# Modulation weights of a two-layer stack: the conditioning product moved from GpSimd and TensorE to VectorE

## The reference

```python
def modulate(h, shift, scale):
    return h * (1.0 + scale) + shift
...
    c_act = jax.nn.silu(c)
    cc_act = jax.nn.silu(c_ctx)
...
        mod = (c_act @ ada_w[l] + ada_b[l])[:, None, :]
        sh1, sc1, g1, sh2, sc2, g2 = jnp.split(mod, N_MOD, axis=-1)
        h = modulate(x, sh1, sc1)
        if need_ctx:
            mod_c = cc_act @ ada_w[l] + ada_b[l]
...
        x = layer_norm(DEEPNORM_ALPHA * x + g1 * y, ln_g[l, 0], ln_b[l, 0])
        h = modulate(x, sh2, sc2)
        x = layer_norm(DEEPNORM_ALPHA * x + g2 * sq_relu_mlp(h, mlp_w1[l], mlp_w2[l]), ln_g[l, 1], ln_b[l, 1])
```

## Time and profile before

| | |
|---|---|
| median of 3 runs | 2835.18 us (2833.04 to 2839.2) |
| profiled execution | 2831.1 us |
| its span | 2829.0 us |
| granted TensorE clock, mean | 0.975 |
| TensorE busy | 2687.7 us, 95% |
| VectorE busy | 1546.7 us, 55% |
| ScalarE busy | 1037.2 us, 37% |
| GpSimd busy | 875.1 us, 31% |

### The profile page before, as it was taken

How to read it: one execution, slowest core, us unless ns; L and a number is a source line. 1 busy time by engine, 2 the same in 40 slices (tenths; PEclk the granted TensorE clock), 3 DMA queues, 4 the chain that set the end, 5 groups by cost and what they waited for, 6 DMA issues and landing times.

```text
span 2829.0 us, 39455 instructions
## 1 busy us (share of the span) xinstructions
PE 2687.7 (95%) x13346; PEld 2210.4 (78%) x13346; DVE 1546.7 (55%) x2275; ACT 1037.2 (37%) x1648; POOL 875.1 (31%) x648
## 2 busy tenths in 40 slices
PE   7999999999999999999989798889999899899997
PEld 6886788887889988888768476678877777788886
DVE  7754554546567755454552774464455655644445
ACT  5234322223347732222331365452233422433323
POOL 2320554543331155445220200144543442300002
PEclk9999999999999999999989899999999999899998
DMA  4121344443300034443412000124444133122222
GB/s 140 67 82 45 127 137 146 140 140 134 133 31 2 2 129 138 141 148 134 142 60 89 8 1 1 52 82 141 135 140 132 69 133 119 62 102 97 97 95 77
DMA packets 77272, 272.27 MB, mean 96 GB/s; under 512 B 8304, under 2 KB 11632, under 8 KB 76784
## 3 DMA queue, kind: packets, MB, share of 16 engines
q1 hardware_dynamic: 58560, 205.55, 21.4%
q10 hardware_dynamic: 18608, 65.34, 6.8%
HBM read 268.75 MB, written 2.10 MB: 96 GB/s over the span
## 4 chain that ended last, share of the span: by engine, by line
PE 80%; DVE 10%; ACT 5%; issue 3%; DMA 1%; POOL 0%; DVEq 0%; ACTq 0%; SPq 0%
PE banks L2175 58%; PE banks L2330 5%; DVE w_lo L1301 3%; PE banks L2627 2%; PE banks L2734 2%; PE banks L2235 2%; PE banks L2719 2%; PE banks L2595 1%; PE banks L2610 1%; ACT w_hi L704 1%; PE banks L2364 1%; PE banks L2699 1%; DVE ffn_hid L2099 1%; DVE attn_nm L1922 1%; PE banks L2624 0%
## 5 line engine op out<-in xcount | busy, mean ns | idle before, releaser
L2175 PE MATMUL banks<-h_hi,w_hi 128*128 128x512 f32 x1616 | 644.9, 399 | 26.8 <-DVE w_lo L1301 21.3
L2175 PE MATMUL banks<-h_lo,w_hi 128*128 128x512 f32 x1616 | 633.2, 392 | 0.0
L2175 PE MATMUL banks<-h_hi,w_lo 128*128 128x512 f32 x1616 | 631.8, 391 | 0.0
L704 ACT ACTIVATE w_hi<-w_raw 128x1024 fp32r<-128x1024 f32 x371 | 389.8, 1051 | 573.6 <-PE banks L2175 452.9
L1301 DVE TENSOR_TENSOR w_lo<-w_raw,w_hi 128x1024 fp32r<-128x1024 f32 x371 | 522.3, 1408 | 140.6 <-ACT w_hi L704 127.7
L2175 PE MATMUL banks<-g_hi,w_hi 128*128 128x512 f32 (+1 forms) x1120 | 437.7, 391 | 13.4 <-DVE w_lo L1301 8.7
L2175 PE MATMUL banks<-g_lo,w_hi 128*128 128x512 f32 (+1 forms) x1120 | 429.2, 383 | 0.0
L2175 PE MATMUL banks<-g_hi,w_lo 128*128 128x512 f32 (+1 forms) x1120 | 428.5, 383 | 0.0
L520 POOL TENSOR_TENSOR ada_raw<-ada_raw,c_act 128x1024 f32<-128x1024 f32 x112 | 220.9, 1972 | 646.3 <-DMA ada_raw<-ada 646.0
L2175 PEld LDWEIGHTS banks<-h_hi,w_hi 128*128 128x128 f32 x1616 | 305.3, 189 | 103.3 <-DVE w_lo L1301 31.9
L2175 PEld LDWEIGHTS banks<-h_hi,w_lo 128*128 128x128 f32 x1616 | 305.2, 189 | 65.0
(11 more groups left out here) (398 smaller groups left out, 3704.8 us busy)
## 6 DMA issues: line engine op xcount, KB each, us to landing
w_raw<-weights SPq DMA_DIRECT2D x384, 512.0 KB, 3.2
ada_raw<-ada ACTq DMA_DIRECT2D x112, 512.0 KB, 3.4
x<-x SPq DMA_DIRECT2D x4, 512.0 KB, 6.8
out<-x SPq DMA_DIRECT2D x8, 256.0 KB, 2.2
mix_cum<-ret_tab ACTq DMA_DIRECT2D x1, 1024.0 KB, 4.9
nsa_w<-cmp_w ACTq DMA_DIRECT2D x1, 1024.0 KB, 7.2
nsa_cbias<-nsa_cbias ACTq DMA_DIRECT2D x1, 1024.0 KB, 9.6
attn_ctx<-ctx ACTq DMA_DIRECT2D x1, 1024.0 KB, 6.8
```

What stands on the lines that cost most here:

```text
L704: act.activation(w_hi[s][:], w_raw[s][:], ACT.Copy).then_inc(w_hi_done, 1)
L2175: mm = pe.matmul(bank, w[s][:, k, :], m[:, k, :], start=(n == 0 and a == 0), stop=(n == kts - 1 and a == 2))
```

## The change

A job's weights are laid out the other way round: the 128 outputs lie on the partitions and the 1024 inputs along the row. The SiLU of `c` and `c_ctx` is then wanted as a row that is the same on all partitions: `c_row` (128 x 2 x 1024), loaded already repeated, with the SiLU on ScalarE (`silu_of_rows`). It lies in memory that other stages overwrite, so it is loaded again, `c` alone, before out1 and before out2. A job becomes one instruction of VectorE, `tensor_tensor_reduce` with product and sum into `ada_col` (128x1), and the addition of the bias from there. GpSimd's and TensorE's parts are taken out.

Places move too: nsa_in and attn_in carry no jobs any more, nor do the first pair of out1 and the second pair of mlp0_up0; in their stead all 4 pairs of ffn0_down2, 2 of ffn1_down2 and 2 of mlp0_down3 carry one. In a pair the load is issued behind ScalarE's first split, and VectorE's part comes between the second split and the second body, in front of which it waits for the load. In out0, out1 and mlp0_up0 ScalarE runs the SiLU before the second body of a pair, in out0 and out1 with the table of the square root loaded again behind it. The core of the diff:

```diff
-ADA_STAGES = ["out0", "nsa_in", "out1", "attn_in", "conv_in"]
-ADA_STAGES += [n for n, _ in PLAN if (n[:3] == "ffn" and n[4:] != "_down2") or (n[:4] == "mlp0" and n[4:] != "_down3")]
-ADA_FIRST = {"attn_in": 6, "mlp0_up0": 1, "conv_in": 1}
+ADA_STAGES = ["out0", "out1", "conv_in"] + [n for n, _ in PLAN if n[:3] == "ffn" or n[:4] == "mlp0"]
+ADA_FIRST = {"out1": 1, "mlp0_up0": 2, "conv_in": 1}
+ADA_PAIRS = {n: {"ffn1_down2": 2, "mlp0_down3": 2}.get(n, PAIRS[n] - ADA_FIRST.get(n, 0)) for n, _ in PLAN
+             if n in ADA_STAGES}
...
-            def condition(a, who):
-
-                pool.wait_ge(ada_loaded, 16 * a + 16)
-                vector = c_act[:, :, who:who + 1].broadcast_to([P, KT, P])
-                pool.tensor_tensor(ada_raw[:], ada_raw[:], vector, ALU.mult).then_inc(ada_step, 1)
...
             def load_ada(...):
-                    act.wait_ge(ada_added, a + 1)
+                    if not isinstance(a, int) or a > 0:
+                        act.wait_ge(ada_done, a)
...
+            def silu_of_rows(rows, n):
+
+                act.wait_ge(row_in, 16 * n)
+                act.activation(rows, rows, ACT.Silu).then_inc(c_silu, 1)
...
                 with act.Fori(p0, p1 - tail) as i:
                     for s in range(2):
                         split_next(i, s)
-                        if s:
+                        if s == 0:
                             load_ada(name, i, first)
...
             first_residual = scaled_squares(1, "ffn0")
-            table_of_sqrt()
             p0 = PAIR0["out0"]
+            load_ada("out0", p0, 0)
             first_residual(p0, 0, 0)
             split_next(p0, 1)
-            load_ada("out0", p0, 0)
+            silu_of_rows(c_row[:], 1)
+            table_of_sqrt()
             first_residual(p0, 1, 1)
...
+                    if not isinstance(a, int) or a > 0:
+                        dve.wait_ge(ada_taken, a)
+                    dve.wait_ge(ada_loaded, 16 * a + 16)
+                    dve.tensor_tensor_reduce(ada_raw[:], ada_raw[:], c_row[:, who, :], 1.0, 0.0, ALU.mult, ALU.add,
+                                             ada_col[:]).then_inc(ada_done, 1)
                     dve.wait_ge(ada_done, a + 1)
-                    dve.tensor_scalar(mod[:, bass.ds(a - skipped, 1), who], psum[5][:, 0:1],
+                    dve.tensor_scalar(mod[:, bass.ds(a - skipped, 1), who], ada_col[:],
...
                 with dve.Fori(p0, p1 - tail) as i:
                     for s in range(2):
                         split_next(i, s)
+                        if s:
+                            take_ada(name, i, first)
                         body(i, s, 2 * (i - PAIR0[name]) + s)
-                    take_ada(name, i, first)
...
-            def ada_unit(name, i, first):
-
-                if with_ada(name, first):
-                    a = i - ada_skipped(name)
-                    pe.wait_ge(ada_added, a + 1)
-                    if not isinstance(a, int) or a > 0:
-                        pe.wait_ge(ada_taken, a)
-                    pe.matmul(psum[5][:, 0:1], ada_sum[:, 0, :], ones[:, 0:1], start=True, stop=True)\
-                        .then_inc(ada_done, 1)
```

More of the change, by code:

```diff
@@ L75 @@
 assert _c == ADA_JOBS and ADA_JOB0["ffn0_up1"] == ADA_CTX
-ADA_BEFORE_NSA = ADA_JOB0["nsa_in"] + 4
-ADA_BEFORE_ATT = ADA_JOB0["attn_in"]
+ADA_BEFORE_ATT = ADA_JOB0["mlp0_up0"]
 def with_ada(name, first=0):
-    if name not in ADA_JOB0 or name == "nsa_in" and first > 3:
+    if name not in ADA_JOB0:
         return False
-    return first == 6 if name == "attn_in" else first >= ADA_FIRST.get(name, 0)
+    return 0 <= first - ADA_FIRST.get(name, 0) < ADA_PAIRS[name]
 def ada_skipped(name):
```

159 lines of the change are left out of this document (70 added, 89 removed).

## The result

| | before | after |
|---|---|---|
| median of the runs | 2834.15 us (2833.04 to 2839.2) | 2795.11 us (2790.92 to 2801.81) |
| ratio, 95% interval | | 0.9861 (0.9842 to 0.988) |
| profiled execution, its span | 2831.1, 2829.0 | 2797.2, 2795.4 |
| TensorE busy | 2687.7 | 2660.7 |
| VectorE busy | 1546.7 | 1595.2 |

The account below looks back on a forecast made before the run. TensorE's matmuls, and its waits for the low halves of weights made by VectorE, were taken as the bound. 26.2 + 17.8 - 11.4 = 32.6 us off 2831.1 gave 2798.5 profiled, a median of 2802.6, range 2791 to 2825.

Parts of the forecast that it names:

- TensorE's matmul, 26.2 us: On TensorE in all pairs with jobs: removing 112 jobs at 0.234 us each saves 26.2 us.
- GpSimd beside VectorE, 17.8 us: First MLP, conv_in and elsewhere: VectorE no longer slowed by GpSimd, saving 8.0, 6.8 and 3.0 us, 17.8 in all.
- elsewhere: Openings of nsa_in, attn_in and the ffn stages: 3.0 us saved, an estimate bounded by 0 and 6.
- The length of the product-and-sum, 1.24 us: On VectorE, each job: the new instruction over 128x1024 takes 1.24 us, in a block of 1.55 us.
- the case of the half rate: Rival, VectorE: product-and-sum some 2.3 us, blocks of 2.6 us, 20 us lost in tight places, 2823 us; chance 0.12.
- Where it is not covered, 11.4 us: Tight stages (ffn0_down2, ffn1_down2, mlp0_down3, out0, others): VectorE's block or ScalarE's SiLU delays TensorE, costing 11.4 us in all.
- Out0 was forecast at 2.2 us: In out0: ScalarE's SiLU and table loads start the second body 2.8 us late; w_lo comes 2.2 us late.
- Out1, mlp0_up0 and the openings, 0.7 forecast: SiLU in out1 and mlp0_up0 and two openings with a block in them: 0.7 us cost together.
- VectorE in GpSimd's place: Rival, MLP and convolution pairs: cover of 0.2 and 0.3 us fails, 14.8 us not won, 2817 us; chance 0.15.
- VectorE as the bound: Rival, VectorE: decides at a block of about 3.0 us; at 3.3 us the kernel is slower, 2852 us; chance 0.03.

Follow-up runs that it names:

- b_no_pool: The kernel before, without GpSimd's product and first two halvings in each job; 2812.31 us against 2831.72, ratio 0.9928.
- after again: The kernel after, unchanged, measured a second time beside three edited versions of it; 2796.57 us against 2833.19, ratio 0.9876.
- the job inside the body: The kernel after, with VectorE's job inside the second residual body in out0, out1 and ffn0_down2; 2791.24 us against 2832.86, ratio 0.9855.
- no product: The kernel after, with the product-and-sum left out of each job; 2784.57 us against 2831.72, ratio 0.9834.
- SiLU early: The kernel after, with the SiLU and square-root table ahead of out0's first residual body; 2795.47 us, ratio 0.9862.

## Why the prediction was right, and where its sizes were off

The forecast was a median of 2802.6 us and a profiled execution of 2798.5; they are 2795.1 and 2797.2. The range of 2791 to 2825 holds both.

**TensorE's matmul, 26.2 us: right, on a condition.** The pairs of the ffn stages are 10.88 us apart, and the one piece of chain in b_no_pool shows the 11.13 with GpSimd idle. Taken out alone the matmul gave 18.4 us, since in the MLP and conv_in the slowed VectorE took the gain back. The term needs the next one to be paid; the prediction added them as if they were independent.

**GpSimd beside VectorE, 17.8 us: right in size, less so in place.** Alone it gave 19.4. In the first MLP it was 9.1 (forecast 8.0), and mlp0 as a whole won 15.1 for 14.3. In conv_in its 11 pairs fall from 129.2 to 11 x 10.92 = 120.1 us: 9.1 for 9.4. (The row conv_in shows 7.6 mainly because it leaves out a pair with a job, whose gain of some 0.9 lies in the row above; that is mainly why mlp0_down3 shows 0.0 there though its own block cost 0.9.) The 3.0 for "elsewhere" were 2.5 in the ffn stages, and another 2.2 came from ffn0_down2 and ffn1_down2, which the sum didn't have; at the openings of nsa_in and attn_in nothing can be told from the noise of their clock.

**The length of the product-and-sum, 1.24 us: right.** It is 1228 ns with both operands in SBUF. So the case of the half rate, which I gave 0.12, is out. The Trainium skill's "Vector Engine (DVE) Microarchitecture Reference", "Points that are easy to get wrong", says that the shape `S2S2D2_STT` with two non-bf16 SBUF sources halves throughput. Applied to this instruction, as the prediction did, it would make some 2.3 us, and the trace doesn't bear that out: 1228 ns in the mean over 112. Whether the instruction has that shape no run shows. The one that took 2.31 us is the one in out0 beside GpSimd. The prediction could have lowered the chance from the trace of before, though not to nothing: a product and sum of two fp32 tensors in SBUF, without an accumulator, takes 0.75 us over 128x512 there, where half the rate would give some 1.3 (an estimate, 512 x 1.07 ns more).

```profile
2285.94 0.75 DVE L2134 SCALAR_TENSOR_TENSOR conv_y<-conv_u,vec,conv_y 128x512 f32 x1 [0.15 <-DVE conv_y L2134]
```

**Where it is not covered, 11.4 us: right by luck in the sum.** The block's part: ffn0_down2 cost 5.8 for 5.9 forecast, ffn1_down2 1.3 for 1.6 (0.7 in the second profile of after), mlp0_down3 0.9 for 1.0 (0.2); the way of counting them, the block straight into a chain in which two engines take turns, was right. Out0 was forecast at 2.2 us and cost 5.6 to 7 (66.2 and 67.5 against 60.6 without job and SiLU). This is the term that was mis-sized, and the steps behind it are three: the product-and-sum met GpSimd's first sum of squares and took 1.1 us longer; the later jobs in out0, which I took as covered, made TensorE wait 0.43 more; and the wait of 2.86 us was followed by a stretch at 1.2 GHz that before does not have there, 1.7 us in one profile (0.28 x 5 + 0.06 x 5, from the clock of 298 to 303 and 303 to 308) and 3 in the other. I had priced the wait and not what TensorE's clock does behind a wait. Out1, mlp0_up0 and the openings, 0.7 forecast, cost some 1.2: one wait of 0.55 in out1, one of 0.24 at the opening of ffn1, and 0.4 in mlp0_up0 (two pairs in 22.2 us, 1871.12 to 1893.31).

**VectorE in GpSimd's place and VectorE as the bound: no.** The block is covered in the MLP pairs by 0.17 us (0.2 forecast), and doubled it still doesn't break the ffn pairs, though it takes 5.0 us from the MLP's.

Stage by stage, the errors of +3.6 us in out0, +1.8 in conv_in, +1.1 in nsa_in and out1, +1.0 in attn_in and out2 and the 3.0 booked elsewhere stand against -3.0 in the two ffn blocks, -1.5 in ffn0_down2, -1.0 each in ffn1_down2 and mlp0_down3, -0.8 in the first MLP, -1.7 in out3 and -1.7 ahead of out0, and cancel. The last two are not the change's, and those of conv_in and mlp0_down3 come in part from the place of the boundary between them. That the whole came out within 1.3 us of the sum is luck. By the medians the gain is 39, 6.5 more than the sum; against its own second measurement (2796.6, ratio 0.9876) it is 35 to 37. What is left of it is within what executions of one kernel differ, 2794.4 to 2802.0 in that measurement with granted clocks from 0.977 to 0.973.

What stays open: whether the two removed costs together are worth 3 or 8 us more than apart. The stages that repeat to 0.1 us show 3, the medians 8 with some 8 of uncertainty.

## What to carry to other kernels

Price an inserted block by the chain it stands in: in a pair bound by TensorE 1.55 us on VectorE cost nothing with 0.2 us of cover, in a stage where ScalarE and VectorE take turns it cost all of its length, and in that stage the same block behind the next addition, inside the wait for the other engine, cost a quarter of it. (In out0 the same move gave nothing.) A small matmul or an engine running beside another is worth its price only if nothing else is late next; measure each alone and both together. And when a stall of some 3 us appears on TensorE, add the time at the low clock behind it.

## What the runs showed of the hardware

**TensorE's clock behind a wait.** In out0 a wait of 2.86, 2.82 and 2.84 us (after, after again, the job inside the body) was each time followed by a stretch at the lower of its two levels, 0.50 granted, 1.2 GHz. In the second profile of after it covers all of 297 to 303, in the first it is shorter (0.72 in the mean of 298 to 303). Waits of 1.38 and of 1.93 with 0.12 (no product, SiLU early) were followed by none. In ffn0_down2 of after TensorE waits 1.94 us at 673.3 and again at 684.4, and the mean clock from 686 to 692 is 0.73; its second profile has such a stretch at 696, behind a third wait. With the jobs of that stage moved away there is none, and with the product-and-sum left out none either. It costs nothing there, since VectorE's chain sets the pace: the products-and-sums start 11.08, 11.07 and 11.10 us apart, the last two of them across that stretch, and TensorE's next wait is 0.98 instead of 1.9. This line of after's busy time by stretch shows it:

```profile
686.00:692.00 6.00, 6.00 (x21) 4.75 (x20) 4.39 (x6) 1.83 (x3) 1.40 (x1) 0.73 0.43 156
```

**Who waits for whom between VectorE and GpSimd.** The product-and-sum that took 2.31 us started at 294.89, 0.1 behind GpSimd's sum (294.79 to 296.12), and ended 1.08 us after that sum's end. The low half that took 1.72 beside a sum of GpSimd shows the same. So does a w_lo of 1.63 us at 671.62 in after: GpSimd's sum had begun at 670.72 and ended at 672.17, and w_lo ended 1.08 later. It looks like waiting for the other instruction's end and then running at full speed; in all of these the time behind that end is 0.1 to 0.2 us less than the instruction takes alone. The Trainium skill, "SBUF — State Buffer", "Who interferes with whom", has it that the pair of ports that the two share is held for a whole instruction by whoever issues first; these rows agree. So what an overlap costs is the rest of the other's instruction, not a share of both: the slowed L2099 of the earlier trace rows started at 1978.78, GpSimd's product ended at 1980.43, and 2.19 is that rest, 1.65, and 0.54.
